# One raw turn at the head of each feed-forward block, and ten tile pairs as block products

## What is computed

```python
def swiglu(h, w1, w3, w2):
    return (jax.nn.silu(h @ w1) * (h @ w3)) @ w2

x = x + 0.5 * swiglu(rms_norm(x, norm_ffn1[l]), ffn1_w1[l], ffn1_w3[l], ffn1_w2[l])
...
x = x + 0.5 * swiglu(rms_norm(x, norm_ffn2[l]), ffn2_w1[l], ffn2_w3[l], ffn2_w2[l])
...
h = rmsnorm(x, g_pre_ffn[l])
gu = h @ w_ffn_in[l]
gate, up = gu[..., :D_FF_2], gu[..., D_FF_2:]
x = x + rmsnorm((jax.nn.silu(gate) * up) @ w_ffn_down[l], g_post_ffn[l])
```

## Time and profile before

| what | us |
|---|---|
| median of 3 runs | 2307.32 |
| lowest and highest | 2301.83 and 2308.82 |
| the profiled execution | 2304.71 |
| its span in the trace | 2302.9 |
| PE busy | 2240.7 (97%) |
| DVE, ACT, POOL busy | 1116.5, 1072.3, 1160.6 |
| mean granted TensorE clock | 0.991 |

### The profile page before, as it was taken

One profiled execution on the slowest core, in us unless ns is written; L12 is line 12 of the kernel. 1 busy time (PEld: TensorE's weight loads), 2 busy tenths in 40 slices (PEclk: granted clock), 3 DMA queues, 4 the chain that ended last, 5 costly groups with the idle time before them and its releaser, 6 DMA issues. The chain is left out here.

```text
span 2302.9 us, 35359 instructions
## 1 busy us (share of the span) xinstructions
PE 2240.7 (97%) x12536; PEld 1889.8 (82%) x12536; DVE 1116.5 (48%) x2070; ACT 1072.3 (47%) x2037; POOL 1160.6 (50%) x723
## 2 busy tenths in 40 slices
PE   7999999999999999999999999999999998999997
PEld 6999888877777789998877776677788877999986
DVE  4887425023431348874253688644511123687611
ACT  5555435145544555553323466644622234555433
POOL 3777457833372457674544422143344444676545
PEclk9999999999999999999999999999999999999999
DMA  4332334322231223333363211021123332233232
GB/s 173 110 101 100 100 93 154 112 72 74 65 101 51 69 92 101 109 101 96 97 155 85 65 38 46 19 73 56 46 91 96 98 97 65 92 109 110 89 93 93
DMA packets 81275, 206.59 MB, mean 90 GB/s; under 512 B 7440, under 2 KB 31120, under 8 KB 80912
## 3 DMA queue, kind: packets, MB, share of 16 engines
q1 hardware_dynamic: 72832, 191.92, 26.3%
q10 hardware_dynamic: 8336, 13.25, 2.0%
HBM read 199.71 MB, written 2.10 MB: 88 GB/s over the span
## 5 line engine op out<-in xcount | busy, mean ns | idle before, releaser
L669 POOL TENSOR_TENSOR parts<-slot,parts 128x512 fp32r<-128x512 f32 (+3 forms) x210 | 379.6, 1808 | 284.1 <-ACT parts L2257 282.4
L694 POOL TENSOR_TENSOR parts<-slot,parts 128x512 fp32r<-128x512 f32 x162 | 229.2, 1428 | 164.3 <-ACT parts L2309 161.7
L2257 ACT ACTIVATE parts<-slot 128x1024 fp32r<-128x1024 f32 (+2 forms) x173 | 157.2, 910 | 312.1 <-PE bank L903 262.5
L898 PE MATMUL bank<-hhi,parts 128*128 128x512 f32 x576 | 226.4, 393 | 5.8 <-ACT hhi L2266 2.7
L899 PE MATMUL bank<-hhi,parts 128*128 128x512 f32 x576 | 225.0, 391 | 0.0
L657 POOL TENSOR_TENSOR parts<-slot,lanes 128x1024 fp32r<-128x1024 f32 x42 | 80.6, 1920 | 245.9 <-PE bank L1798 116.2
L1060 PE MATMUL bank<-hhi,parts 128*128 128x256 f32 x756 | 188.7, 282 | 2.1 <-ACT sc L2353 2.1
L1061 PE MATMUL bank<-hhi,parts 128*128 128x256 f32 x756 | 189.0, 282 | 0.0
L666 POOL TENSOR_TENSOR parts<-slot,parts 128x512 fp32r<-128x512 f32 x55 | 71.3, 1297 | 220.7 <-ACT parts L2257 219.1
L1060 PEld LDWEIGHTS bank<-hhi,parts 128*128 128x128 f32 x756 | 144.1, 191 | 2.7 <-issue 2.6
L903 PE MATMUL bank<-hlo,parts 128*128 128x512 f32 x576 | 144.6, 390 | 0.0
(11 more groups left out here) (680 smaller groups left out, 5959.5 us busy)
## 6 DMA issues: line engine op xcount, KB each, us to landing
slot<-w SPq DMA_DIRECT2D x264, 512.0 KB, 3.7
slot<-w SPq DMA_DIRECT2D x88, 256.0 KB, 2.7
slot<-w SPq DMA_DIRECT2D x48, 448.0 KB, 3.3
hid<-w SPq DMA_DIRECT2D x8, 512.0 KB, 3.5
x<-xT ACTq DMA_DIRECT2D x4, 512.0 KB, 9.8
hid<-headtab ACTq DMA_DIRECT2D x8, 256.0 KB, 3.7
big<-cmpw ACTq DMA_DIRECT2D x4, 512.0 KB, 11.0
hid<-w SPq DMA_DIRECT2D x8, 256.0 KB, 2.7
```

The lines of the kernel that those rows point to most:

```text
L669: pool.tensor_tensor(low, w, high.bitcast(F32), ALU.subtract).then_inc(splits, 1)
L694: pool.tensor_tensor(low, source, high.bitcast(F32), ALU.subtract).then_inc(splits, 1)
L898: pe.matmul(out, high[:, k, :], mhi[:, k, :], start=(start and k == 0), stop=False)
L2257: act.activation(parts[nth % 2][:, 0, 0:kt, :], slot[j][:, 0:kt, :], ACT.Copy).then_inc(highs, 1)
```

## The change

Panels 4 to 7 are no longer made raw: they become the weights of one more turn of block products (9 loop turns and the last, 20 inner tiles). `FFN_UP` now covers panels 0 to 3, of which 2 and 3 go to banks 4 and 5, and `SECOND` is gone. The preparation of the token sums, which was spread over panels 2 to 7, is moved to where panels 2 and 3 run. The third count of `EARLY` is a third loop, of one turn, on ACT and DVE, since the square steps of the memory's norm still belong to eight turns.

```diff
-EARLY = (4, 4)
+EARLY = (4, 4, 1)
-PAIRS = KF // 2 - 3
+PAIRS = KF // 2 - 2
-FFN_UP = dict(products=4, splits=4, highs=4, free0=2, free1=2, silus=2, gscaled=2)
-SECOND = dict(products=4, splits=4, highs=4, free0=1, free1=1, free4=1, free5=1, silus=2, gscaled=2)
+FFN_UP = dict(products=4, splits=4, highs=4, free0=1, free1=1, free4=1, free5=1, silus=2, gscaled=2)
@@ SP, in the stream of loads
-                    n.past(SECOND)
-                    for j in range(RING):
-                        sp.wait_ge(products, n.at("products", j + 1 - RING))
-                        sp.dma_start(slot[j][:, :, :], w8[panel[8] + 2 * RING + j]).then_inc(loaded[j], 16)
-                    panel[8] += 3 * RING
+                    panel[8] += 2 * RING
@@ POOL, ffn
                 n.past(FFN_UP)
-                for nth in range(4):
-                    split(nth, nth, "act")
-                n.past(SECOND)
                 pair_lows()
@@ PE, ffn
                 n.past(RAW)
-                emptied(0, 1)
-                h_panel(2, bank[0][:, :])
-                emptied(1, 1)
-                h_panel(3, bank[1][:, :])
-                n.past(FFN_UP)
-                for nth, b in enumerate((0, 1, 4, 5)):
+                for nth, b in ((2, 4), (3, 5)):
                     emptied(b)
                     h_panel(nth, bank[b][:, :])
-                n.past(SECOND)
+                n.past(FFN_UP)
                 pair_products()
@@ ACT, ffn_up
-                raw_silu(0, 0, 1)
-                high_part(3, 3, 2)
                 for k in range(HK):
                     gained(k, g)
-                high_part(4, 0, 3, load=2)
-                raw_silu(1, 0, 2)
-                high_part(5, 1, 4, load=2)
-                n.past(FFN_UP)
+                high_part(3, 3, 2)
+                raw_silu(0, 0, 1)
                 for k in range(HK, KD):
                     gained(k, g)
-                high_part(2, 2, 1)
-                raw_silu(0, 0, 1)
-                high_part(3, 3, 2)
-                n.past(SECOND)
+                n.past(FFN_UP)
@@ DVE, ffn_up
                 raw_gate(0, 0, 1)
+                token_sum(0)
                 raw_hidden(0, 1, 0, 2, 1)
-                token_sum(0)
-                raw_gate(1, 0, 3)
-                raw_hidden(1, 1, 1, 4, 2)
-                n.past(FFN_UP)
                 for a in range(1, 4):
                     token_sum(a)
-                raw_gate(0, 0, 1)
-                raw_hidden(0, 1, 2, 2, 1)
...
-                raw_hidden(1, 5, 3, 4, 2)
-                n.past(SECOND)
+                raw_hidden(1, 5, 1, 4, 2)
+                n.past(FFN_UP)
...
-                pair_turn(4 + 2 * done, True)
+                pair_turn(2 + 2 * done, True)
```

More of the change, by code:

```diff
@@ L3369, in ffn_up @@
                 for nth, turns in enumerate(EARLY):
-                    events = {**PAIR_TURN, **(dict(msteps=2) if loads else {}), **({} if nth else dict(hhis=1, hlos=1))}
+                    events = {**PAIR_TURN, **(dict(msteps=2) if loads and nth < 2 else {}), **({} if nth else dict(hhis=1, hlos=1))}
                     with n.turns(dve, turns, events) as i:
-                        pair_turn(i * 2 + (4 + 2 * done), squared=i + done if loads else None, early=None if nth else i)
+                        pair_turn(i * 2 + (2 + 2 * done), squared=i + done if loads and nth < 2 else None,
+                                  early=None if nth else i)
                     done += turns
```

## The result

The changed kernel takes **2320.7 us** in the median of six runs (2315.7 to 2323.8), the kernel before 2304.1 us in the same session (2299.8 to 2308.8). The ratio is 1.0068, 95% interval 1.0055 to 1.0081: slower by 0.7%, or 16.6 us. The profiled execution took 2316.65 us with a span of 2314.9 us, against 2304.71 and 2302.9: +12.0 us between the two that can be compared line by line.

What follows compares the result with a forecast made beforehand. PE, 97% busy, was taken to bound the kernel. Products save 5.4 us and new waits behind DVE's chain cost 17.4, so +12.0 on the 2307.3 us median gives 2319 us; the range is 2312 to 2327 us.

Steps and rivals of the forecast that it cites:

- What goes and comes: Per layer, four raw panels go (21.76 us) and one loop turn comes (19.95 us): -1.81 us, -5.4 us in all.
- ACT up to the eighth gained tile: Second head: ACT's copy of rinv ends at 829.10, and its following steps complete the eighth gained tile at 836.97.
- DVE's chain: Second head, behind the gained tiles: sums 3.80 us, then 8.91 us from first weight sum to sum_low, without idle.
- The three waits: PE idles about 3.9, 2.0 and 0.6 us before next_first, next_fifth and pair(0), released by POOL, DVE and DVE.
- the slack that the prediction gave it: Some 2 us before next_fifth could start, so a slow next_first costs nothing.
- The wait before panel 2 of the first head: PE's wait for bank 0 there goes with the new banks, but shortens nothing that is late.
- The sum: Heads' net losses of +4.24, +4.25 and +3.51 us give +12.0: products save 5.4, new waits cost 17.4.
- The rival in which the cover holds: ACT and DVE finish preparation as panel 3 ends, giving -5.4 us, 2302 us; chance 0.03.
- The shorter chain: Rival: undisturbed DVE operations or earlier ACT steps save 2 us a head, 6 us less, 2313 us; chance 0.10.
- The term that I took at nothing: PE's slow clock behind the heads' waits: 0 to 9 us in all; as rival 4.5 us more, 2324 us, chance 0.13.
- The prediction's own signs of being wrong: pair(0) sooner than 20 us after the copy, a turn over 20.1, or first-turn matmuls at twice their usual step.

Runs made afterwards that it cites:

- e1: Changed kernel plus one unused DVE operation per head between the token sums and the first weight sum; 2323.31 us, ratio 1.0081.
- e2: Changed kernel plus one unused POOL operation per head ahead of the first quarter's low part; 2321.38 us, ratio 1.0069.
- e0: The changed kernel run again without an edit, as base of the first session; 2321.19 us, ratio 1.0069 to the kernel before.
- e3: Changed kernel plus unused matmuls filling PE's idle time in each head, 20 before next_first and 4 before next_fifth; 2314.08 us, ratio 1.0041.
- e4: Changed kernel with each head's first weight sum on DVE moved ahead of three token sums; 2316.49 us, ratio 1.0048.
- e6: Changed kernel with the moves of e4 and e5 together; 2314.66 us, ratio 1.0041.
- e8: e6 with ACT making the high parts of weight quarters earlier, so POOL works during DVE's token lows; 2322.66 us, ratio 1.0075.
- e5: Changed kernel with the fourth token sum, second gate and second hidden tile moved behind sum_low, their ACT steps later too; 2318.51 us, ratio 1.0050.

## Why the prediction was right, and where it was off

**What goes and comes.** As put. The added turn takes 19.95 us in the profile, the rest of the loops grow by 19.91 to 19.95 in each layer, and the third loop costs nothing.

**ACT up to the eighth gained tile.** Forecast 7.87 us behind the end of the copy, and the sums 0.03 later. DVE's three sums start at 841.80, 7.82 behind the copy's end at 833.98.

**DVE's chain.** Forecast 3.80 us for the sums and 8.91 from the weight sum to the start of sum_low, with no idle between. Measured 3.80 (841.80 to 845.60) and 8.80 (845.60 to 854.40), with none. This is the step on which everything hung, and e1 shows it: 1.14 us more on DVE are 1.13 us more at PE, in the head where the clock is undisturbed. The head is 21.84 us instead of 22.03 where the clock is full.

**The three waits.** Forecast 3.9, 2.0 and 0.6 us. The brackets name DVE's token low and DVE's sum low for the second and third, as forecast. For the first they name no engine, but POOL's quarter ends 0.11 us ahead of next_first, in the changed kernel and again in e2, where it was made a microsecond later. The brackets give 3.72, 0.53 and 0.30 in the second head and 2.89, 1.76 and 0.31 in the third. They count from the modelled end of a matmul, which lies 0.16 us behind the start that could follow it (0.39 long at a spacing of 0.227, 0.28 at 0.12), so that 3.72 is 3.88 in the way the forecast counted, 1.76 is 1.92 and 0.30 is 0.46. The third head waits less before next_first because its raw panels end later. In the second the missing 1.2 us before next_fifth are the slow next_first, which used the slack that the prediction gave it. The wait before panel 2 of the first head, which was said to go with the new banks, did not: it is 2.71 us, for POOL, where it was 1.62, for DVE. It costs nothing, since DVE's chain ends later.

**The sum.** Forecast +12.0, measured +12.0 in span and in time between the profiled executions. That they agree to the tenth is luck: the work and the waits come to +11.4 where 12.0 were forecast (DVE's chain is 0.2 us shorter in each head), the slow clock and the load in the first layer 1.4 more, and 0.8 us less stand elsewhere. The rival in which the cover holds needed the third token low by 842.5, 14.0 us behind the copy of rinv; it was complete at 853.16, 19.8 us behind it, where 19.9 were forecast. The shorter chain did not appear either: the 1.78 us operation of the earlier trace rows is 1.77 again, because POOL's second quarter stands beside it as before.

**The clock, mis-sized.** The medians are 16.6 and 15.4 us apart, not 12. The term that I took at nothing, with 0 to 9 us as bounds, is where the prediction is off. The changed kernel's runs have a granted clock of 0.985 to 0.990, those of the kernel before 0.990 to 0.993 in e0's session; and within the six runs of e0 the time falls from 2323.95 us at 0.984 over 2319.6 at 0.988 to 2315.85 at 0.990. A head and turn in which it falls cost from nothing or 0.9 us (changed kernel) over 1.9 (e0) to 1.4 and 2.2 (e1, behind waits of 4.01 and 5.21 us). The prediction's own signs of being wrong did appear, in one head of three: the first turn of the first layer takes 21.07 us, over the 20.1, and its first seven matmuls are spaced at 0.21 us instead of 0.12. Three or four microseconds in the median would have been the better value, which makes 2323 from the same start (how the 3 to 5 us of the medians divide between the heads and the rest of the kernel isn't shown); that the forecast of 2319 came within 2 us owes something to its start, the median of 2307.3 of the runs then at hand, where the larger samples say 2304 to 2306. The Trainium skill, page "TensorE: Matmul & The Clock Gate", section "HAM oscillation — how this bites in real kernels", says that gaps between matmul batches bring the throttle back; the windows of e0 and e3, with 0.50 and 1.00 of the clock behind the same place, agree. Why the clock falls in some heads and not in others isn't shown by any run: the third head of the changed kernel, with waits of 2.89 and 1.76 us, kept it, and the first, with 0.98 and 1.76, did not.

**What else was possible.** The prediction didn't ask whether the order of the new head could be better. e4 to e6 give part of the answer: the preparation on DVE and POOL between the last gained tile and the end of the first turn stays about the same amount, and moving it mostly moves the stall. The head can be cut to 19.5 us, and the sum of head and first turn only from 41.9 to 41.3 (without the slow clock). To break even the sum would have to fall to 38.1, the mean head of before, 37.98, with its turn of 20.05, less the added turn of 19.95.

## What to carry to other kernels

Work that is removed from the bounding engine was also somebody's cover: add up what the other engines still have to do between the same two events, in order, and compare that chain with what is left of the cover, before the saving is counted. Where that chain is on one engine, moving its links behind the first consumer only pays if the next turn has room on the same engine. And a POOL operation started earlier is not free if DVE is working from SBUF at that time (e8). Last, look at the clock in the stretch before a small gain or loss is put down to an edit: in e4 and e5 it hid most of what DVE's shorter chain had won.

## What the hardware showed that I had not expected

DVE and POOL hold each other up by up to about the length of the other's operation when DVE reads two inputs from SBUF. Beside POOL operations of 128x512: 1.22 us become 2.32 and 2.28 (e8), 0.68 become 1.76 (e2), 1.66 and 1.75 (e6); POOL's 1.27 become 2.27. In the first head of e4 the weight sum starts beside a POOL operation of 128x1024, and its 0.70 us become 2.88:

```profile
31.19 2.88 DVE L3226 TENSOR_TENSOR bank<-slot 128x512 f32<-128x512 f32 x1
...
31.04 2.47 POOL L664 TENSOR_TENSOR parts<-slot,parts 128x1024 fp32r<-128x1024 f32 x1 [1.55 <-ACT parts L2244]
```

DVE operations with one input in PSUM kept 0.68 to 0.70 us beside POOL operations of 128x512. The Trainium skill, page "SBUF — State Buffer", section "Who interferes with whom", says that such a DVE instruction contends with a GpSimd instruction that reads SBUF, that the port pair which the two share is an exclusive lock, and that a DVE instruction with at most one SBUF input doesn't contend. All three agree with these rows. For the lock the last pair speaks most clearly: the POOL operation, which started first, keeps the 2.4 to 2.5 us that it has elsewhere and ends at 33.51, and DVE's ends 0.56 us behind it, as if it had run afterwards. By that, the 1.04 and 1.78 us of the earlier trace rows were never the operation's own length: e4 has it once undisturbed, with 0.68 us:

```profile
850.93 0.68 DVE L3203 TENSOR_TENSOR silu_r<-hid,o_sb_r 128x512 fp32r<-128x512 f32 x1
```

The second surprise is how far the clock of a kernel that is 97% busy moves the time by itself: without any edit, runs of the kernel before lie between 2299.8 and 2309.9 us, and of the slow stretches in which the profiles of e0 and e3 differ, three stand hundreds of microseconds from the change.
